# A two-layer encoder trunk on one core: the first maxima product of a slot moved behind the scores

## What is computed

```
def block_attention(q, k, v, scale):
    def one(qblk):
        s = jnp.einsum('bqhgc,bkhc->bhgqk', qblk, k).astype(jnp.float32) * scale
        p = jax.nn.softmax(s, axis=-1).astype(v.dtype)
        return jnp.einsum('bhgqk,bkhc->bqhgc', p, v)

def trunk(x, ...):
    for layer in range(DEPTH):
        if layer % 2 == 0: x = even_layer(...)   # dilated + latent heads, gate, output projection
        else:              x = odd_layer(...)    # grouped heads, gate, output projection
```

## Time and profile before

| | us |
|---|---|
| median of 3 runs | 2059.51 |
| lowest and highest | 2058.98, 2059.64 |
| span of the profiled execution | 2057.7 |
| PE busy in it | 2020.9 (98%) |
| DVE, ACT, POOL busy in it | 1201.7, 1127.7, 953.7 |

### The profile page before, as it was taken

The page is one execution under the profiler, slowest core; times in us unless marked ns, Lnnn a source line. Parts: engine busy times, 40 slices in busy tenths (PEclk is TensorE's granted clock), DMA queues, the critical chain, the costliest instruction groups (busy, mean ns, idle before and its releaser), DMA issues.

```text
span 2057.7 us, 25552 instructions
## 1 busy us (share of the span) xinstructions
PE 2020.9 (98%) x9480; PEld 1629.0 (79%) x9480; DVE 1201.7 (58%) x1935; ACT 1127.7 (55%) x1440; POOL 953.7 (46%) x487
## 2 busy tenths in 40 slices
PE   8999998999999999999999999999999999999998
PEld 6878886888888877777887777888777777777888
DVE  6432135335777666673559777414577778776454
ACT  6142234435666667666446444344677778888431
POOL 1222224434555555556101666433576676677401
PEclk9999999999999999999999999999999999999999
DMA  5133469617655744643435333262223343332535
GB/s 197 54 124 126 155 238 337 166 57 159 128 118 119 177 110 101 149 93 114 153 115 158 135 123 109 94 201 86 80 64 82 76 122 71 80 81 90 170 101 169
DMA packets 172143, 261.38 MB, mean 127 GB/s; under 512 B 78754, under 2 KB 89634, under 8 KB 172020
## 3 DMA queue, kind: packets, MB, share of 16 engines
q1 hardware_dynamic: 172020, 259.76, 44.4%
HBM read 161.78 MB, written 97.92 MB: 126 GB/s over the span
## 4 chain that ended last, share of the span: by engine, by line
PE 90%; DVE 3%; ACT 3%; DMA 2%; issue 1%; POOL 1%; SPq 0%; DVEq 0%; ACTq 0%; POOLq 0%
PE SA L1949 13%; PE OP L1995 11%; PE SM L1875 5%; PE OP L2002 5%; PE OP L533 5%; PE SA L533 5%; PE SM L2048 4%; PE OP L1087 4%; PE SA L2048 4%; PE SA L1087 4%; PE OS L533 3%; PE OS L1995 3%; PE OS L1087 2%; PE OS L2048 2%; PE SM L1871 2%; PE OS L2002 1%
## 5 line engine op out<-in xcount | busy, mean ns | idle before, releaser
L2469 POOL TENSOR_TENSOR c_PL<-c_PF,c_PH 128x1024 fp32r<-128x1024 f32 x128 | 307.8, 2409 | 137.5 <-ACT c_PH L2171 79.8
L2469 POOL TENSOR_TENSOR ab_PL<-ab_PF,ab_PH 128x1024 fp32r<-128x1024 f32 (+3 forms) x128 | 264.6, 2067 | 192.2 <-ACT ab_PH L2171 135.8
L2168 ACT ACTIVATE ab_PF<-SA 128x1024 f32<-128x1024 f32 (+3 forms) x160 | 143.7, 898 | 158.2 <-PE SA L1910 84.8
L2168 ACT ACTIVATE c_PF<-SA 128x1024 f32<-128x1024 f32 x160 | 164.0, 1025 | 85.3 <-PE SA L1949 84.2
L2256 DVE TENSOR_REDUCE c_MH<-SM 128x1 f32<-128x512 f32 x256 | 171.0, 684 | 66.5 <-PE SM L1875 66.4
L431 POOL TENSOR_TENSOR e_wl<-e_raw,e_wh 128x1024 fp32r<-128x1024 f32 (+1 forms) x31 | 73.3, 2363 | 191.5 <-ACT e_wh L600 191.5
L2171 ACT ACTIVATE c_PH<-c_PF 128x1024 fp32r<-128x1024 f32 x128 | 135.8, 1061 | 4.1
L1949 PE MATMUL SA<-c_Q,c_KA 128*128 128x512 f32 x320 | 127.8, 399 | 3.3 <-ACT c_PF L2168 3.3
L1949 PE MATMUL SA<-c_Q,c_KB 72*128 72x512 f32 x320 | 127.1, 397 | 0.0
L1019 POOL TENSOR_TENSOR n_wl<-n_raw,n_wh 128x1024 fp32r<-128x1024 f32 (+1 forms) x24 | 53.8, 2240 | 154.3 <-ACT n_wh L1184 154.3
L1875 PE MATMUL SM<-c_KA,c_Q 128*128 128x512 f32 x320 | 125.1, 392 | 0.0
(11 more groups left out here) (538 smaller groups left out, 5913.0 us busy)
## 6 DMA issues: line engine op xcount, KB each, us to landing
c_Q<-qC_hi SPq DMA_DIRECT2D x32, 384.0 KB, 4.9
e_raw<-in_w_tiles SPq DMA_DIRECT2D x20, 512.0 KB, 3.8
n_raw<-in_w_tiles SPq DMA_DIRECT2D x20, 512.0 KB, 3.8
e_XF<-in_xT SPq DMA_DIRECT2D x12, 512.0 KB, 10.9
silu_gate<-e_ta SPq DMA_DIRECT2D x24, 256.0 KB, 2.1
ab_Q<-qA_hi SPq DMA_DIRECT2D x16, 384.0 KB, 5.5
ab_G<-silu_gate SPq DMA_DIRECT2D x24, 256.0 KB, 3.7
ab_res<-in_xT SPq DMA_DIRECT2D x24, 256.0 KB, 2.9
```

The source lines that it names most:

```text
L2168: nc.scalar.activation(used(PF[p], h, s), used(SA, h, s), ACT.Exp).then_inc(e_done, 1)
L2469: nc.gpsimd.tensor_tensor(used(PL[p], h, s), used(PF[p], h, s), used(PH[p], h, s).bitcast(F32), ALU.subtract).then_inc(p_lo[0], 1)
```

## The change

In latent and grouped heads, a slot's first unit of the next head's maxima is written right behind the scores. Before it stood between the PH products and the PL products. Dilated heads keep their order, and so does the last head of a layer, which has no maxima to make.

```
         for g in range(G):
             h, s = g // NS, g % NS
             units = units_of(h + 1, s) if h + 1 < NH else ()
+            early = h >= NA
             some = len(units) // 2
             scores(h, s)
+            if early:
+                for u in units[:some]:
+                    max_unit(h + 1, u)
             if g >= LAG:
-                pv(g - LAG, units[:some])
-            else:
+                pv(g - LAG, () if early else units[:some])
+            elif not early:
                 for u in units[:some]:
                     max_unit(h + 1, u)
```

## The result

| | before | after |
|---|---|---|
| median, us | 2059.57 (4 runs, 2058.98 to 2060.04) | 2067.02 (4 runs, 2065.32 to 2068.87) |
| the same kernels on another occasion | 2058.82 (21 runs, 2056.68 to 2061.07) | 2065.97 (5 runs, 2065.24 to 2067.01) |
| span of the profiled execution | 2057.7 | 2063.7 |

The ratio of after to before is 1.0039 (95% interval 1.0027 to 1.0052), on the second occasion 1.0035 (1.0023 to 1.0048). By the medians the kernel became 7.1 to 7.5 us slower; the forecast was 8.6 (2068.1, range 2063.5 to 2072).

The account below looks back on a forecast made before the run. PE, busy 98% of the span, was taken as the bound. Waits of 5.7 (slot 4), 0.9 (head 0) and 2.0 us (slot 6) sum to 8.6, with latent heads and spacing at 0: 2068.1 us, range 2063.5 to 2072.

Parts of the forecast that it names:

- PE is the path: Whole kernel: PE, busy 98% of the span, sets the pace; a moved product costs the same, only waits change the time.
- Slot 4: Grouped heads: the moved load waits for a reduction behind a cast; 0.41 us in each of 14 heads, 0.87 in head 0.
- Slot 6: Grouped heads: same pattern; 0.29 us each in heads 8 to 14, 2.0 us together, free by 0.08 in heads 1 to 7.
- rival 1: Grouped heads: DVE doesn't gain on PE or head 0's disturbance goes on; 12.3 us lost, 2071.8 us; chance 0.12.
- The cast is long for POOL's sake: Slot 3 of grouped heads: the cast takes 1.30 us beside POOL's subtraction, against 0.68 in slot 5 without one.
- Latent heads: no wait: Latent heads 8 to 14: the moved load, behind six score products, finds its bank free; 0, at most 0.1 us.
- Spacing: All 220 changed slots: the new product order is worth about 0.01 us a slot either way; taken as 0, +-2.2 us.
- Dearer: Grouped heads, slot 6: costs 0.11 us each in heads 1 to 7, 0.70 in heads 8 to 14; 2071.8 us; chance 0.12.
- not slower, by spacing: Changed slots: new neighbours close gaps between products; at 0.04 us a slot the loss is gone, 2059.3 us; chance 0.06.
- no wait ends last: Moved load: it isn't held back as read, or the bank is free earlier; 2059.5 us, within 2 us; chance 0.07.
- the clock: Grouped heads: short waits lower PE's clock for one slot in each of 15 heads; +42 us, 2110 us; chance 0.01.
- What would show it: Trace after: PE waits at line 1875 in grouped slots 4 and 6; slots 4 last 3.19 us, slots 6 3.08, latent unchanged.

Follow-up runs that it names:

- e7: The changed kernel, but in slot 4 of grouped heads the product stands where it stood before; grouped heads +6.8 us in all against the kernel before.
- e8: The changed kernel without the second half of POOL's low-part subtraction in slot 2 of grouped heads 1 to 15; grouped heads +4.5 us against before.

## Why the prediction was right, step by step

- *PE is the path, so a moved product costs nothing and a wait costs its full length.* Right of the waits, less the 0.13 that is free. A moved product did cost or gain a little, by spacing (below). Each part alone moved the median by about what its slots give: grouped +9.4 against +9.1, latent -1.2 against -1.5.
- *Slot 4: 0.41 in 14 heads, 0.87 in head 0.* The slots grew by 0.42 and 0.90. The parts held as well: 0.06 from the end of a reduction to the load (measured 0.05), 0.33 to the next product (0.34), 0.13 of lateness free (0.12 to 0.13 over all longer waits).
- *Slot 6: 0.29 in heads 8 to 14, nothing in heads 1 to 7, since DVE gains on PE.* Measured 0.28 and -0.01; e7 shows that the gain is real, against rival 1. The sum for heads 1 to 7 leaves out a term: a cast at 1618.50 and a reduction 0.60 later end it at 1619.78, not 1619.81. The missing 0.03 stands between ACT's end and the cast (1618.10 and 1618.13 after), and nothing hangs on it.
- *The cast is long for POOL's sake.* Right. The prediction had it from two rows of different slots; e8 shows it, and the casts of heads 0 and 15 show that it is a wait.
- *Latent heads: no wait.* Right.
- *Spacing: 0 +-2.2.* This is the term that was mis-sized: -1.5 in the latent heads and +0.5 in the grouped ones (+0.6 in the other slots, -0.1 in those slots 6 that lost nothing), -1.0 in all. The forecast stood 1.1 too high, and 1.0 of it is this. The bound of 0.01 a slot, taken from two grouped slots, was too narrow for the latent heads, where six slots in ten gave 0.026 to 0.028; the two slots hadn't the new order in them at all. That the error came to 1 us in all is in part luck, as the two kinds of heads went opposite ways.
- *Rivals.* "Dearer" came nowhere; "not slower, by spacing" has its mechanism, at a ninth of the size it needed; "no wait ends last" and "the clock" are out: the granted clock was 1.00 over the latent and over the grouped heads in all ten profiles.
- *What would show it.* PE's own rows list one of the 22 waits, PEld's all of them: that sentence named the wrong row. "The latent heads' slots as long as before" was wrong too (-0.21 a head). The lengths of slots 4 and 6 and the load's start (0.05 after the reduction's end, 0.53 after its place) came as stated.

## What to carry to other kernels

An operation moved forward in one engine's queue gets nothing if what releases it stands in another engine's queue behind something tied to the same moment; look in that queue for what is ahead of the releaser, and move that first. For each place the loss can be worked out beforehand from four numbers of the trace: end of the releaser, delay to the load, distance from a late load to the next product, and where that product would have been. A loss upstream has to be carried along, since the releaser's engine gains by it (slot 6 here). If the writer of a bank pair is moved, move its reader too: here moving the reduction on DVE gave back 8.4 of the 9.1 us. It gained nothing over before, where PE had no such wait to lose.

## What the runs showed of the hardware

- In these 512-column products a weight load that started up to about 0.13 us late cost nothing, and a later one its lateness beyond that (0.08 late, 0.00 lost; 0.30 late, 0.17 lost; 0.53 late, 0.40 lost; 1.03 late, 0.90 lost).
- A DVE cast from SBUF to SBUF of 128 x 1024 took 1.30 us with a POOL subtraction at work when it began and 0.68 to 0.69 without. It was held rather than slowed: it ended 0.55 us after POOL's subtraction, whether they had overlapped by 0.58, 0.75 or 1.21 us. With POOL's work over 0.36 us before the cast's start the excess vanished.
- The order of the same fourteen products changed their total by up to 0.028 us, the same in latent heads 9 to 14 and in every profile with the move in them, with no wait listed. Which neighbours cost what stays open.
